# Scores of two of three attention branches from stacked high and low parts, placed by DMAs inside the SBUF

## What is computed

```python
ya = forgetting_attention(qa, ka, va, logf)                 # branch A, 8 heads of 64, no rotation
qb_rot, k_sel, k_win = rope(qb), rope(ksb), rope(kwb)
yb = nsa_attention(qb, qb_rot, k_cmp, v_cmp, k_sel, v_sel, k_win, v_win, gates)  # branch B
qc, kc = rope(qc), rope(kc)
yc = differential_attention(qc, kc, vc, lam, lam_init, g)   # branch C, 4 heads, two softmax maps each
merged = g0 * (ya @ w_br_a) + g1 * (yb @ w_br_b) + g2 * (yc @ w_br_c)
x = x + merged @ w_out
x = x + sigmoid(x @ w_ple_gate) * (p @ w_ple)
```

## Time and profile before

| | us |
|---|---|
| median of 3 runs | 1540.33 |
| lowest, highest | 1539.79, 1542.48 |
| the profiled execution, its own time | 1538.75 |
| span of its records | 1536.9 |
| PE busy | 1496.8 |
| DVE, ACT, POOL busy | 941.2, 636.7, 75.4 |

### The profile page before, as it was taken

How to read it: one execution, slowest core, us unless ns; L and a number is a source line. 1 busy time by engine, 2 the same in 40 slices (tenths; PEclk the granted TensorE clock), 3 DMA queues, 4 the chain that set the end, 5 groups by cost and what they waited for, 6 DMA issues and landing times.

```text
span 1536.9 us, 22588 instructions
## 1 busy us (share of the span) xinstructions
PE 1496.8 (97%) x7957; PEld 1205.0 (78%) x7957; DVE 941.2 (61%) x2197; ACT 636.7 (41%) x1499; POOL 75.4 (5%) x80
## 2 busy tenths in 40 slices
PE   8999999999999999999999999999999999999997
PEld 6777777887787777888787787787887777778885
DVE  6866765655657776554576667655556677854544
ACT  6533434433344444343444334334334444434343
POOL 1000000000000010000100000000000011000011
PEclk9999999999999999999999999999999999999998
DMA  7223332222223333332342324222222233233321
GB/s 197 84 83 90 97 76 62 56 70 62 69 63 96 90 83 83 98 108 72 106 108 69 103 76 115 64 52 66 63 62 76 70 96 89 70 101 99 89 86 72
DMA packets 250301, 129.50 MB, mean 84 GB/s; under 512 B 45690, under 2 KB 245972, under 8 KB 250196
## 3 DMA queue, kind: packets, MB, share of 16 engines
q1 hardware_dynamic: 250196, 128.13, 31.2%
HBM read 118.67 MB, written 2.10 MB: 79 GB/s over the span
## 4 chain that ended last, share of the span: by engine, by line
PE 87%; DVE 6%; ACT 3%; issue 2%; DMA 0%; POOL 0%; SPq 0%; ACTq 0%; POOLq 0%; DVEq 0%
PE D L732 24%; PE D L734 22%; PE D L733 22%; PE Ob L920 7%; PE S L879 5%; PE T L898 4%; DVE w_lo L1293 2%; ACT w_hi L1059 1%; PE Mb L936 1%; ACT probs L1173 1%; PE Mb L846 1%; PE Ob L924 1%; PE Mb L813 1%; DVE y_lo L1627 1%; DMA acc<-in_x_dram 0%
## 5 line engine op out<-in xcount | busy, mean ns | idle before, releaser
L732 PE MATMUL D<-h_hi,w_hi 128*128 128x512 f32 x1264 | 542.1, 429 | 9.9 <-DVE zs L1444 3.7
L734 PE MATMUL D<-h_lo,w_hi 128*128 128x512 f32 x1264 | 495.9, 392 | 0.0
L733 PE MATMUL D<-h_hi,w_lo 128*128 128x512 f32 x1264 | 494.3, 391 | 0.0
L1293 DVE TENSOR_TENSOR w_lo<-raw,w_hi 128x512 fp32r<-128x512 f32 (+2 forms) x504 | 295.0, 627 | 310.9 <-ACT w_hi L1059 310.7
L1059 ACT ACTIVATE w_hi<-raw 128x512 fp32r<-128x512 f32 (+2 forms) x504 | 264.6, 572 | 306.7 <-PE D L734 305.4
L732 PEld LDWEIGHTS D<-h_hi,w_hi 128*128 128x128 f32 x1264 | 238.5, 189 | 69.3 <-issue 18.4
L1173 ACT ACTIVATE probs<-probs,nmax 128x128 f32<-128x128 f32 (+3 forms) x256 | 141.9, 555 | 355.0 <-DVE nmax L1545 354.9
L734 PEld LDWEIGHTS D<-h_lo,w_hi 128*128 128x128 f32 x1264 | 237.4, 188 | 52.9
L733 PEld LDWEIGHTS D<-h_hi,w_lo 128*128 128x128 f32 x1264 | 239.4, 189 | 30.8 <-issue 0.5
L1545 DVE CUSTOM_DVE_ANT_0 probs<-S,maskb 128x128 f32<-128x128 f32 (+3 forms) x256 | 115.1, 487 | 48.4 <-PE S L879 29.8
L540 DVE COPY pT<-T 128x128 f32<-128x128 f32 (+3 forms) x160 | 77.4, 486 | 48.0 <-PE T L898 47.5
(11 more groups left out here) (243 smaller groups left out, 1498.9 us busy)
## 6 DMA issues: line engine op xcount, KB each, us to landing
raw<-in_w_in_dram SPq DMA_DIRECT2D x124, 512.0 KB, 3.9
raw<-in_w_in_dram SPq DMA_DIRECT2D x32, 256.0 KB, 3.7
raw<-in_w_out_dram SPq DMA_DIRECT2D x16, 512.0 KB, 4.1
raw<-in_w_ple_gate_dram SPq DMA_DIRECT2D x16, 512.0 KB, 4.2
rs<-rx SPq DMA_DIRECT2D x80, 64.0 KB, 2.0
raw<-in_cmp_w_k_dram SPq DMA_DIRECT2D x8, 512.0 KB, 3.8
raw<-in_cmp_w_v_dram SPq DMA_DIRECT2D x8, 512.0 KB, 3.8
raw<-in_w_br_a_dram SPq DMA_DIRECT2D x16, 256.0 KB, 2.9
```

Source lines behind the costliest of these rows:

```text
L732: pe.matmul(o, w_hi[:, sl, cs], hi[:, k, :], start=(k == 0), stop=False)
L733: pe.matmul(o, w_lo[:, sl, cs], hi[:, k, :], start=False, stop=False)
L734: ins = pe.matmul(o, w_hi[:, sl, cs], lo[:, k, :], start=False, stop=last)
L1293: TT(w_lo[:, sl, half], raw[:, ring(L, t, RAW), half], f(w_hi[:, sl, half]), ALU.subtract).then_inc(M["dve_lo"], 1)
```

## The change

For branches B and C the scores are made in another form. For each head a query buffer of 128 rows (`q_st`) holds the high part in one half of its rows and the low part in the other, and the key buffers hold the high part of a head in both halves, and the low part of it in both halves. Then two matmuls of 128 rows for each head give (high + low) by high and (high + low) by low: four matmuls in place of six. Branch A keeps its six and two. The wait for the scores' bank is now before each head's matmuls rather than one for both.

To get there, the rotation writes its high part to `rx` and its low part to `rs` (`new_hi`, `new_lo`), and a new item `put`, 12 groups after the tile's end, copies them to their rows by DMAs of 64 rows (128 KB each): 4 for a query tile, 8 for a key tile. Half of these are issued by SP, the other half by ACT, which issued none before; both first wait for the low part (`qk_s`), for the scores that still read the buffer (`pe_s`), and for `kwb`, whose place overlaps `flat`, for the end of tile `w1v` 3 (`pe_dense`). PE's first scores of a unit wait for the DMAs (`put_s`), and so do ACT's copy of the next rotated tile into `rx` and SP's next swap into `rs`. POOL works in place in `rs`; `rb` is gone; `vbd` has room of its own, and its zeroing in each layer is gone. In stage 3 `kwb` and `vsb` change places.

```diff
-    st[3] = [("qb", 0), ("w1v", 0), ("kwb", 0), ("w1v", 1), ("za", 3), ("w1v", 2), ("vsb", 0), ("w1v", 3), ("vwb", 0)]
+    st[3] = [("qb", 0), ("w1v", 0), ("vsb", 0), ("w1v", 1), ("kwb", 0), ("w1v", 2), ("za", 3), ("w1v", 3), ("vwb", 0)]
...
                 follow.append([8, ("swap", t)])
                 follow.append([11, ("rot", t)])
+                follow.append([12, ("put", t)])
...
+        def places(kind, n):
+            src = (rx, rs)
+            if kind[0] == "q":
+                return [(q_st[n % 2][h][half((h + part_) % 2), :], src[part_][half(h), :]) for h in range(2) for part_ in range(2)]
+            at = {"ksb": KS, "kwb": KW, "kc": KC[n % 2]}[kind]
+            return [(part(at + 2 * h + part_)[half(g), :], src[part_][half(h), :])
+                    for h in range(2) for part_ in range(2) for g in range(2)]
+
+        def place(M, eng, t, which):
+            kind, n, _ = tiles[t]
+            eng.wait_ge(M["qk_s"], rots.after(t))
+            if kind == "kwb":
+                eng.wait_ge(M["pe_dense"], tile_of[("w1v", 3)] + 1)
+            elif kind != "ksb":
+                eng.wait_ge(M["pe_s"], rows_before[(4 if kind == "qb" else 8) + n - 1])
+            for dst, src in places(kind, n)[which::2]:
+                eng.dma_start(f(dst), src).then_inc(M["put_s"], 16)
...
@@ sync
-                                sp.wait_ge(M["pool_rot"], n - 1)
+                                sp.wait_ge(M["put_s"], put_before[tiles[it[1]][:2]])
...
+                        if it[0] == "put":
+                            place(M, sp, it[1], 0)
...
@@ gpsimd
-                            pool.tensor_tensor(rb[:], rs[:], sinT[:], ALU.mult).then_inc(M["pool_rot"], 1)
+                            pool.tensor_tensor(rs[:], rs[:], sinT[:], ALU.mult).then_inc(M["pool_rot"], 1)
...
@@ tensor
+                                at = {"c": KC[u % 2], "sel": KS, "win": KW}[m]
+                                for h in range(2):
+                                    pe.wait_ge(M["dve_max"], r - 1 + h)
+                                    qx = q_st[b][h][:, qs]
+                                    pe.matmul(Sc[h][:, 0:n], qx, part(at + 2 * h)[:, 0:n], start=True, stop=False)
+                                    pe.matmul(Sc[h][:, 0:n], qx, part(at + 2 * h + 1)[:, 0:n], start=False, stop=True).then_inc(M["pe_s"], 1)
...
@@ scalar
-                                    act.wait_ge(M["sw_ld"], 64 * (r - 1))
                                     act.wait_ge(M["dve_rm"], r - 1)
+                                    act.wait_ge(M["put_s"], put_before[(kind, n)])
...
-                            if u is not None and u >= 2:
-                                act.wait_ge(M["pe_s"], rows_before[u - 1])
-                            A(hi_, rc[:], ACT.Copy).then_inc(M["act_rot"], 1)
+                            A(new_hi, rc[:], ACT.Copy).then_inc(M["act_rot"], 1)
+                        elif what == "put":
+                            place(M, act, it[1], 1)
```

More of the change, by code:

```diff
@@ L307, in hybrid_trunk @@
                 hids.add(kind)
-        elif it[0] == "rot":
-            qk_ready.add(tiles[it[1]][:2])
+        elif it[0] == "put":
+            placed.add(tiles[it[1]][:2])
         elif it[0] in ("vt", "gates", "ht", "kcmp", "vcmp", "cs", "ct", "Y"):
@@ L399, in hybrid_trunk, with half @@
         w_lo = sb("w_lo", [P, SPL, 8 * P], F32R)
-        at_arena = -(-nc.sbuf_base // 32) * 32
         arena = sb("arena", [P, 16 * S], F32R)
-        vbd = nc.alloc_sbuf_tensor_at("vbd", [P, 2, P], F32, offset=at_arena + 12 * S * 4)
         def part(n, k=1):
             return arena[:, n * S:(n + k) * S]
-        q_hi, q_lo = [part(0), part(1)], [part(2), part(3)]
-        k_hi, k_lo = [part(4), part(5)], [part(6), part(7)]
-        ks_hi, ks_lo, kw_hi, kw_lo = part(8), part(9), part(10), part(11)
+        def half(h):
+            return slice(HD * h, HD * h + HD)
+        q_hi, q_lo = [part(0), part(2)], [part(1), part(3)]
+        k_hi, k_lo = [part(4), part(6)], [part(5), part(7)]
+        q_st = [[part(2 * b + h) for h in range(2)] for b in range(2)]
+        KC, KS, KW = (4, 8), 8, 12
         flat_both = part(12, 4).rearrange("p (m c) -> p m c", m=16)
@@ L450, in hybrid_trunk @@
         hid = y_f[:, 2, :].rearrange("p (a g b c) -> p a g b c", a=2, g=2, b=4)
+        vbd = sb("vbd", [P, 2, P])
         kcmpT = sb("kcmpT", [P, 2 * C32])
@@ L556, in landed_at @@
             return slot_sum[t % RAW] + 16 * ((t - T0) // RAW + 1)
-        def rot_dst(kind, n):
-            if kind == "ksb":
-                return ks_hi, ks_lo, None
-            if kind == "kwb":
-                return kw_hi, kw_lo, None
-            u = (4 if kind == "qb" else 8) + n
-            return (k_hi[u % 2], k_lo[u % 2], u) if kind == "kc" else (q_hi[u % 2], q_lo[u % 2], u)
+        def places(kind, n):
[8 more added lines that the diff above has]
+            eng.wait_ge(M["qk_s"], rots.after(t))
+            if kind == "kwb":
+                eng.wait_ge(M["pe_dense"], tile_of[("w1v", 3)] + 1)
[3 more added lines that the diff above has]
+                eng.dma_start(f(dst), src).then_inc(M["put_s"], 16)
+        put_sum, at_ = {}, 0
+        for x_ in placed.order:
+            at_ += 16 * len(places(*x_))
+            put_sum[x_] = at_
+        put_before = {x_: put_sum[x_] - 16 * len(places(*x_)) for x_ in put_sum}
         with nc.Block() as block:
@@ L865, in _ @@
                                 elif m == "c":
[L866 to L871, removed]
-                                      "sel": (ks_hi, ks_lo), "win": (kw_hi, kw_lo)}[m]
+                                    pe.wait_ge(M["put_s"], max(put_sum[("qc", u - 8)], put_sum[("kc", u - 8)]))
+                                elif u > 4:
+                                    pe.wait_ge(M["put_s"], put_sum[("qb", u - 4)])
+                                else:
+                                    pe.wait_ge(M["put_s"], max(put_sum[("qb", 0)], put_sum[("ksb" if m == "sel" else "kwb", 0)]))
@@ L873, in _ @@
                             n = (i + 1) * P
                             qs = slice(i * P, n)
-                            for step, (qx, kx) in enumerate(((q_hi[b], ka), (q_lo[b], ka), (q_hi[b], kb))):
-                                last = step == 2 and m != "a"
-                                for h in range(2):
-                                    ps = slice(HD * h, HD * h + HD)
-                                    ins = pe.matmul(Sc[h][:, 0:n], qx[ps, qs], kx[ps, 0:n], start=(step == 0), stop=last)
-                                    if last:
-                                        ins.then_inc(M["pe_s"], 1)
@@ L882, in _ @@
-                            if m == "a":
-                                for h in range(2):
-                                    ps, hh = slice(HD * h, HD * h + HD), 2 * u + h
+                            if m == "a":
+                                if r >= 2:
+                                    pe.wait_ge(M["dve_max"], r)
+                                for step, (qx, kx) in enumerate(((q_hi, k_hi), (q_lo, k_hi), (q_hi, k_lo))):
+                                    for h in range(2):
+                                        pe.matmul(Sc[h][:, 0:n], qx[b][half(h), qs], kx[b][half(h), 0:n], start=(step == 0), stop=False)
+                                for h in range(2):
+                                    ps, hh = half(h), 2 * u + h
@@ L1097, in _ @@
                             act.wait_ge(i_ang, ANGLE_STEPS)
[L1098 removed]
+                            A(cosT[:], rs[:], ACT.Sin).then_inc(i_act, 1)
                             A(rc[:], rx[:], ACT.Sin).then_inc(i_act, 1)
@@ L1529, in _ @@
                             t = it[1]
-                            hi_, lo_, u = rot_dst(*tiles[t][:2])
                             r = rots.after(t)
```

37 lines of the change are left out of this document (16 added, 21 removed).

## The result

The changed kernel takes 1609.6 us (median of 4 runs, 1603.2 to 1613.6), the kernel before in the same comparison 1540.1: a ratio of 1.044, with an interval from 1.042 to 1.046. I had forecast 1557, with a range up to 1583. The direction was right, the size was not: 69 us slower, not 17. The profiled execution took 1603.2 us with a span of 1601.3, 64.4 us more than the span before. In two of the experiments one execution each was far slower than the others (1843.7 and 2935.1 us); the medians there are of the other executions.

A forecast was written before the change was run, and what follows sets the result against it. PE was taken to bound the kernel, busy 1496.8 of 1536.9 us. 1538.75 - 19 (scores) + 38 (stalls behind ACT's puts) = 1557.8 us, taken as 1557, with a range of 1529 to 1583.

The forecast's parts named there:

- The gain on PE: Score pairs of branches B and C: four full-height matmuls cost PE less than six half-height ones, -19 us (-17 to -21).
- ACT's issue: Each DMA issue holds ACT 0.62 us: 1.25 us for a query tile, 2.5 us for a key tile.
- The rival of full turns: SP and ACT take turns at issuing, so key puts hold ACT 5 us: 1589 us, slower, chance 0.12.
- The stalls: PE waits because work behind ACT's puts comes late: 18.9 us a layer, +38 us for two.
- the walk through the lists: For each of a layer's 14 puts: low part's end, ACT's hold and work behind it, against when PE needs it.
- The clock: PE's clock after a stall: the prediction had no term for it.
- The short hold: An issue holds ACT only a small part of 0.6 us, or engines catch up sooner: 1530 us, faster, chance 0.28.
- The rival of the row groups: Old half-height matmuls overlap, so the new pairs cost PE more than the old: 1592 us, slower, chance 0.02.

The follow-up runs named there:

- the pair of kernels: POOL issuing ACT's share, `kc` copied into branch B's free buffer: with four full-height score matmuls 1525.3 us, with six of half height 1541.2 us.
- the last kernel: The changed kernel with POOL issuing ACT's share of the puts and `kc` copied out into branch B's free buffer: 1525.3 us, ratio 0.990.

## Why the prediction was wrong

The prediction's sum was 1538.75 - 19 + 38 = 1557.8 us for the profiled execution. With what was measured it is 1538.75 - 17.4 + 59.0 + 22.8 = 1603.2. Two steps failed: the sum of the stalls was 21 us too small, and what PE's clock does after a stall was put at nothing, without a reason.

**The gain on PE** (19 us, 17 to 21): right, at the lower end; 17.4 by busy time, 16 by the pair of kernels. Its reason was misread, though. The prediction has the two halves of the old form overlap "only in part". Two moments of the pair of the earlier trace rows, in the trace of the kernel before:

```profile
371.15 0.40 PE L879 MATMUL S<-arena 64*128 64x512 f32 x2
371.39 0.39 PE L879 MATMUL S<-arena 64*128 64x512 f32 x2
```

Each row is two matmuls, one for each head, and takes no longer than one: they start 3 to 4 ns apart. So the six cost three distances, 0.69 us. The other 0.40 of the pair's 1.09 is in four distances, the one ahead of it, two of the three from step to step, and the one behind it, of 0.32 to 0.34 us in place of 0.23; what makes them longer no run shows. The new form needs four distances instead of three and has none of these long ones. That the pairs get cheaper was read rightly from the rows; but the gain lies in the long distances that go away, not in the smaller number of matmuls.

**ACT's issue** (0.62 us each): right for a query tile, whose hold is 1.14 us (I had 1.25). For a key tile I had 2.5 us and measured 3.0 to 3.4; without SP beside it, it is 2.4. The rival of full turns (5 us) was wrong. The Trainium skill, page "Perfetto Trace Analysis", section "DMA Instruction — HWDGE (DVE, Sync)", has two sequencers lock one descriptor block; the rows show a part of that, 0.6 to 1.0 us per key tile, where taking turns would have cost 2.5.

**The stalls** (18.9 us a layer): this sum failed, by more than 10. What PE waited at each place, less what it waited there before:

```
place     forecast   layer 0   layer 1
ksb          2.0       2.9       2.5
qb 0         2.1       2.1       2.1
kwb          3.9       4.8       4.9
qc 0         1.4       2.3       2.3
kc 0         1.9       2.7       2.8
qc 1         1.9       4.7       5.6
kc 1         1.3       0.8       0.0
qc 2         0.0       2.7       2.6
kc 2         1.6       1.4       1.4
qc 3         0.0       2.5       2.6
kc 3         2.8       2.5       2.4
sum         18.9      29.4      29.2
```

The sum of both layers is 58.6 us, all of PE's additional idle time but 0.4. Eight of the eleven places are within 1.3 us of the forecast; there the walk through the lists held up. `ksb`, `kwb` and `kc` 0 are 0.5 to 1.0 above it, about what the longer hold adds; but the later `kc` tiles have the same hold and are not above it, so this is not shown.

Three places carry 8 to 9 of the 10 us a layer. At **`qc` 1** the walk went to the wrong consumer. I followed DVE's delay to the copy of the gate tile and to PE's tile at 476.59, but four microseconds before that PE takes `y_lo`. The trace of the kernel before has this row, and I had not read it:

```profile
472.57 0.47 PE L732 MATMUL D<-y_hi,w_hi 128*128 128x512 f32 x1 [0.20 <-DVE y_lo L1627]
```

PE already waits there, so that there was no slack at all, and the whole delay goes to PE, 4.7 us. Of this 0.4 is `y_lo` itself, which took 1.65 us here and 1.24 before. At **`qc` 2 and 3** I had 0.3 us to spare. The landing took 4.2 us and not 3.6, and it also moved POOL's product, which waits for the swap, onto DVE's weights. DVE's and POOL's timelines in stage 9, of the changed kernel and then of the kernel before:

```profile
537.42 1.62 POOL L705 TENSOR_TENSOR rs<-rs,sinT 128x512 f32<-128x512 f32 x1 [10.17 <-DMA rs<-rx]
...
537.81 2.38 DVE L1313 TENSOR_TENSOR w_lo<-raw,w_hi 128x512 fp32r<-128x512 f32 x2
```

```profile
511.40 1.70 POOL L684 TENSOR_TENSOR rb<-rs,sinT 128x512 f32<-128x512 f32 x1 [6.75 <-DMA rs<-rx]
...
513.81 1.29 DVE L1293 TENSOR_TENSOR w_lo<-raw,w_hi 128x512 fp32r<-128x512 f32 x2 [1.85 <-ACT w_hi L1059]
```

The same two operations take 2.38 us beside POOL's and 1.29 after it: 1.1 of the 2.7 us. That this is the cause rests on these rows; no run takes POOL's product away.

**The clock** (nothing): the step that was missing altogether, 22.8 us, as much again as the miss in the stalls and more than the gain. I priced a stall at its length. In the trace of the kernel before no stall within the run is followed by a lower clock, so no row there gave a price; but its waits within the run are 1.9 us at most, and I forecast some of 2 to 5. What PE does after such a wait was an unknown cost, to be bounded and put into the range. With dense distances of 0.23 us at one level, the other level, 1.2 GHz, would have given 0.46 as the upper bound; the rows above have 0.43.

**Which rival.** The short hold fell: ACT's issues last what SP's do. Its time of 1530 was close to what the change gives when ACT does not issue and nothing waits for landings. The full turns fell. The rival of the row groups fell as a price, since the new pair of 512 keys costs 0.91 us, less than the old, although the overlap it rests on is there. In sum, by runs: 55 us leave with ACT's issues (1609.6 to 1554.6) and 29 more with the landings (to 1525.3), the clock contained in both. These 84 us are the loss of 69 and the 15 by which the last kernel is faster than the one before.

## What to carry to other kernels

That an engine is busy for only 40% of the time doesn't make a DMA issue on it free if its list is walked in order: cost the hold at the very place, and give the issues to an engine whose list has room (here SP: 51 us). A buffer that DMAs still read must not be the one into which the next result is copied out; a second buffer was worth 21 to 36 us. And price a stall of PE at more than its length: here 59 us of idle time took 23 us of clock with it.

When walking a delay through the lists, look for the first consumer, not for the one that the chain happens to name, and take every place with a wait already, however small, as one without slack.

## What the runs showed of the hardware

- The granted clock fell to half after a wait of PE of 2.3 us (`qc` 0 in layer 0) and even around one of 1.9 (for `y_q`, at the end of both layers), and not after others of 2.3 to 2.8 (`qc` 0 and `kc` 0 in layer 1), nor after the same wait of 1.9 in the profiled execution of the kernel before. The same kernel so has different times: 1603 to 1614 us, with a mean clock of 0.981 to 0.975.
- Other executions of the kernel before have a mean clock down to 0.993 where the profiled one has 0.997, and spans up to 1541.4 us in place of 1536.9. So its small spread goes with the clock too.
- Matmuls of 64 rows in the upper and the lower half of the array start 3 to 4 ns apart and take no longer than one; a pair of 512 keys made of six such costs 0.40 us more than its three distances.
- An issue takes 0.60 us on SP alone and 0.62 us on ACT alone in the median (single ones up to 1.84 and 1.06), and up to 1.24 us on ACT when SP issues too; on POOL it takes 0.52 us.
- DMAs of 128 KB from buffer to buffer land 2.3 us after their issue when one engine issues them, and 3.2 to 3.4 us after it when two do (medians).
- DVE operations with two inputs beside a POOL product took 1.8 times as long: 2.38 us for two in place of 1.29.
